# Attention's row sums: reciprocal on VectorE from PSUM in place of logarithm and exponential on ScalarE

## The reference, cut to what matters

```
log_f = log_sigmoid(f_logit + b_f);  c = cumsum(log_f)
logits = q.k / sqrt(d) + c[t] - c[s]         (causal)
probs = softmax(logits)
o = probs @ v
y = (o * silu(g)) @ w_out
```

## Time and profile before

| | us |
|---|---|
| median of 3 runs | 2958.67 (2952.82 to 2960.47) |
| the profiled execution | 2953.92 |
| its span in the trace | 2952.1 |
| TensorE busy | 2819.0 (95%) |
| VectorE busy | 1713.6 (58%) |
| ScalarE busy | 1064.9 (36%) |
| GpSimd busy | 1349.7 (46%) |

### The profile page before, as it was taken

How to read it: one execution, slowest core, us unless ns; L and a number is a source line. 1 busy time by engine, 2 the same in 40 slices (tenths; PEclk the granted TensorE clock), 3 DMA queues, 4 the chain that set the end, 5 groups by cost and what they waited for, 6 DMA issues and landing times. The chain is left out here.

```text
span 2952.1 us, 39371 instructions
## 1 busy us (share of the span) xinstructions
PE 2819.0 (95%) x13294; PEld 2181.5 (74%) x13294; DVE 1713.6 (58%) x2184; ACT 1064.9 (36%) x1407; POOL 1349.7 (46%) x1652
## 2 busy tenths in 40 slices
PE   5999999998999999999989999999999999996997
PEld 3788888866878877787778888777676777774775
DVE  7679989988262612663564223263566666667454
ACT  5343443444120100000233222132466666665232
POOL 2344544557754534445724233577422222223775
PEclk9999999999999999999999999999999999998998
DMA  7521111155321132113221111323300000000423
GB/s 301 181 70 63 63 65 67 68 182 175 136 68 54 40 131 78 43 44 106 100 93 36 37 36 36 121 95 89 116 29 30 28 28 30 32 30 8 161 81 115
DMA packets 89450, 241.15 MB, mean 82 GB/s; under 512 B 6960, under 2 KB 20352, under 8 KB 88576
## 3 DMA queue, kind: packets, MB, share of 16 engines
q1 hardware_dynamic: 59648, 172.58, 17.8%
q10 hardware_dynamic: 29696, 67.16, 6.3%
HBM read 207.20 MB, written 32.51 MB: 81 GB/s over the span
## 5 line engine op out<-in xcount | busy, mean ns | idle before, releaser
L630 PE MATMUL ps<-t_h_hi,t_wh 128*128 128x512 f32 x2464 | 1003.7, 407 | 42.9 <-POOLq L542 15.4
L632 PE MATMUL ps<-t_h_hi,t_wl 128*128 128x512 f32 x2464 | 979.5, 398 | 0.0
L631 PE MATMUL ps<-t_h_lo,t_wh 128*128 128x512 f32 x2464 | 977.6, 397 | 0.0
L534 POOL CAST t_wh<-t_wst 128x1024 fp32r<-128x1024 f32 (+2 forms) x306 | 317.6, 1038 | 1431.3 <-PE ps L632 1318.9
L539 POOL TENSOR_TENSOR t_wl<-t_wst,t_wh 128x256 fp32r<-128x256 f32 (+2 forms) x1224 | 935.7, 796 | 24.5
L630 PEld LDWEIGHTS ps<-t_h_hi,t_wh 128*128 128x128 f32 x2464 | 465.8, 189 | 199.9 <-issue 52.6
L632 PEld LDWEIGHTS ps<-t_h_hi,t_wl 128*128 128x128 f32 x2464 | 465.8, 189 | 112.9
L631 PEld LDWEIGHTS ps<-t_h_lo,t_wh 128*128 128x128 f32 x2464 | 466.3, 189 | 111.4 <-issue 6.0
L2257 DVE SCALAR_TENSOR_TENSOR ps<-t_upad,t_vec,ps 128x1024 f32<-128x1024 f32 x224 | 275.5, 1286 | 7.1 <-DVE ps L2251 0.9
L630 PE MATMUL ps<-t_y_hi,t_wh 128*128 128x512 f32 x512 | 205.1, 401 | 11.0 <-POOLq L542 8.9
L632 PE MATMUL ps<-t_y_hi,t_wl 128*128 128x512 f32 x512 | 204.0, 398 | 0.0
(11 more groups left out here) (344 smaller groups left out, 3850.7 us busy)
## 6 DMA issues: line engine op xcount, KB each, us to landing
t_wst<-w_even_in SPq DMA_DIRECT2D x40, 512.0 KB, 3.3
t_wst<-w_ple SPq DMA_DIRECT2D x64, 320.0 KB, 2.8
t_wst<-w_even_out SPq DMA_DIRECT2D x32, 512.0 KB, 3.5
t_wst<-w_fox_in SPq DMA_DIRECT2D x32, 512.0 KB, 3.5
t_modw<-w_mod SPq DMA_DIRECT2D x6, 2048.0 KB, 16.1
t_xr<-x_d ACTq DMA_DIRECT2D x6, 2048.0 KB, 13.2
t_wst<-w_gla_in SPq DMA_DIRECT2D x24, 512.0 KB, 3.6
t_wst<-w_odd_in_a SPq DMA_DIRECT2D x16, 512.0 KB, 3.5
```

What stands on the lines that cost most here:

```text
L534: pool.tensor_copy(wh[b][:, 0:w], wst[b][:, 0:w]).then_inc(S("w_high"), 1)
L630: pe.matmul(o, w1, x1, start=start and k == 0, stop=False)
L631: pe.matmul(o, w1, x2, start=False, stop=False)
L632: last = pe.matmul(o, w2, x1, start=False, stop=stop and k == kts - 1)
```

## The change

ScalarE's two operations are taken out, with their semaphore f_ln. In their place VectorE has one, `shares`, which reads bank 5 and writes the reciprocal to the same buffer as before. It stands right behind `gated` of the same half. TensorE's `weight_sums` waits for f_inv in place of f_ln. Nothing else moves.

```diff
@@ TensorE, weight_sums
-            at_least("f_ln", 2 * p + c)
+            at_least("f_inv", 2 * p + c)
@@ ScalarE
-        def sums(p, c):
-            act.wait_ge(S("f_ws"), 2 * p + c + 1)
-            act.wait_ge(S("f_pv"), 12 * p + (12 if c else 4))
-            A(share_of(c)[:, :], bank(5), ACT.Ln).then_inc(S("f_ln"), 1)
-
-        def shares(p, c):
-            act.wait_ge(S("f_ln"), 2 * p + c + 1)
-            A(share_of(c)[:, :], share_of(c)[:, :], ACT.Exp, scale=-1.0).then_inc(S("f_inv"), 1)
@@ ScalarE, window
             scores_out(p, 3, 0)
-            if carry:
-                sums(p - 1, 1)
-                shares(p - 1, 1)
             tops_out(p, 0, 0)
...
                 next_square(n, 0)
-            sums(p, 0)
             tops_out(p, 1, 1)
...
                 next_raw(n, 1)
-            shares(p, 0)
             if more:
                 next_square(n, 1)
@@ ScalarE, behind the last window
         window(7, more=False)
-        sums(7, 1)
-        shares(7, 1)
-        act.wait_ge(S("f_inv"), 16)
@@ VectorE
+        def shares(p, c):
+            dve.wait_ge(S("f_ws"), 2 * p + c + 1)
+            dve.wait_ge(S("f_pv"), 12 * p + (12 if c else 4))
+            dve.reciprocal(share_of(c)[:, :], bank(5)).then_inc(S("f_inv"), 1)
@@ VectorE, window
             below_max(p, 2, 0)
             if carry:
                 gated(p - 1, 1)
+                shares(p - 1, 1)
             below_max(p, 3, 1)
...
             gated(p, 0)
+            shares(p, 0)
             below_max(p, 7, 0)
@@ VectorE, behind the last window
         gated(7, 1)
+        shares(7, 1)
         shared(7, 1)
```

More of the change, by code:

```diff
@@ L380, in build @@
     RED = numbered((0, 0), (0, 1), (1, 1), (1, 0))
-    LN = numbered((0, 0), (1, 0))
-    INV = numbered((0, 0), (1, 0))
     YG = numbered((0, 0), (1, 0))
```

## The result

The changed kernel takes 2983.45 us (median of 4 runs, 2981.99 to 2986.45), the kernel before 2955.74 us (4 runs, 2952.73 to 2960.47). The ratio is 1.0098, 95% interval 1.0082 to 1.0114: slower by 27.7 us, where 12.5 were forecast: the right way, and more than twice the sum. (2983.45 still lies in the stated range, just under its upper end of 2984; but that range was set on a median of 2958.67 for the kernel before, and the four runs have 2955.74.)

What follows compares the result with a forecast made beforehand. TensorE was taken to bound the six loop windows, other engines window 7. Terms 8.4 + 1.0 + 3.1 = 12.5 us, set on the median 2958.67, gave 2971.2 us; range 2957 to 2984, the forecast case's own 2968 to 2976.

Steps and rivals of the forecast that it cites:

- the stated range: Forecast of the whole time: 2957 to 2984 us, taking in the upper half of the cheap case and all the dear one.
- the 18 loads and the 7 that move: ScalarE's table loads: 18 go, 23.1 us; 7 in windows 0 to 6 move to next_ln.
- place two: First half, windows 0 to 7: shared 1.4 us late, covered by 3.5 us slack in windows 0 to 6; window 7 pays.
- window 7's middle: From gated(7, 0) to TensorE's weight sums: hardly any wait to cover the reciprocal, so the whole 3.1 us is paid.
- the tail: After the last gated: 0.1 us gained, off the path as TensorE waits for GpSimd's split; counted as 0.
- Window 7's head: Carried half in window 7: ScalarE and the maxima 2.6 us late; cost taken as 1.0 us, between 0 and 2.6.
- The reciprocal's length: Each 128x512 reciprocal on VectorE out of PSUM: 3.15 us taken, between 0.77 and 8.1 us.
- the third rival: In the list of rivals: TensorE's clock falls from 2.4 to 1.2 GHz, about 18 us, 2989 us; chance 0.05.
- the second: Dearer reciprocal: eight ordinary turns an element, 4.34 us each, costing 21.5 us, 2980.2 us in all; chance 0.20.
- place one: Carried half, windows 1 to 7: delay 3.07 us less cover 1.65; six windows pay 8.4 us, window 7 1.0 us.

Runs made afterwards that it cites:

- both reciprocals hidden: Changed kernel with both reciprocals moved to stretches where VectorE waits anyway (carried one at the window's head): 2954.70 us, ratio 1.0001 to the kernel before.
- the half c = 0 alone: Changed kernel with the carried half (c = 1) back on ScalarE's logarithm and exponential, reciprocal only for c = 0: 2956.08 us, ratio 1.0009 to the kernel before.
- The variant with a buffer of its own: Changed kernel with a separate buffer for the share of c = 1, so scores_out(p, 4) no longer waits for shared(p - 1, 1): 2957.47 us, ratio 1.0007.
- the variant with the reciprocal behind the subtractions: Changed kernel with the carried reciprocal moved behind the four subtractions, right ahead of shared(p - 1, 1): 2969.12 us, ratio 1.0057 to the kernel before.
- the last variant: Changed kernel, carried reciprocal behind the four subtractions, plus two copies of the bank to an unread buffer before shared: 2977.17 us, ratio 1.0079.

## Why the prediction was wrong

**Right.** What bounds the kernel and which way it goes; that relieving ScalarE is worth nothing (period 73.20 with both reciprocals hidden); the 18 loads and the 7 that move (counts of both match; ScalarE's relief of 42.7 us was 41.0); that all hangs on the carried half, through `scores_out(p, 4)` and TensorE's scores, where most of the wait stands before unit 6 (2.64 us) and the rest before unit 7 (0.36); that place two is covered in windows 0 to 6; window 7's middle, 3.1 us forecast, 3.2 measured (3.0 with the half c = 0 alone); the tail, 0 forecast and 0.0 measured.

**Right by luck.** Window 7's head, 1.0 us forecast and 1.0 measured. The 1.0 was picked between 0 and 2.6 without a count, and the way to it went through ScalarE's late `scores_out`. The variant with a buffer of its own has no such wait and pays the same (26.47 against 26.45 us from gate to maxima), so it did not hang on that wait; in both TensorE waits some 2.7 us for VectorE's maxima, before the change 0.72. No run here isolates it further.

**The reciprocal's length**, taken as 3.15 us, is 3.35: by the three sizes 253 ns (16 columns), 1.75 us (256) and 3.35 us (512) it has the fixed part of its neighbours (0.15 us) and 6.2 ns a column; the 2.55 us of 384 columns lie on the same line. That is a fifth of a microsecond too little, 1.2 us over six windows. The Trainium skill's "repeat count of 8" ("VectorE: DVE Perf Modes", "First, the fixed hardware budget") taken as eight turns an element would have made 4.3 us. The page gives no duration, and that reading is mine; the measurement decides: a column takes as long as about six of an ordinary operation (6.24 / 1.03). (The prediction calls this case the third rival at one place; it is the second.)

**The step that failed** is the sum of place one: "3.07 - 1.65 = 1.42 us", six times 1.4. It lacked two terms.

First, 1.5 to 1.6 us a window, some 9.8 us in all. I let the work behind the reciprocal move by the reciprocal's length and keep its own. The four subtractions had ended 0.13 us before GpSimd's split began (2378.70 and 2378.83), and moved on top of it they double (the expectations call them "of 128 columns"; two of them have 384). I had read that effect in window 7, and priced it there; in the loop I did not look what GpSimd does in the microseconds into which the work was being pushed.

Second, 9.6 us for the clock. I had it as a rival with 0.05, argued away from waits of 0.80 and 1.08 us at a clock of 1.00, "near to" a stall of 1.4. For a stall of that length the argument held: with 1.16 + 0.37 us the clock stayed at 1.00 in all six windows. But the stall was 2.64 + 0.36 us, twice as long, because of the first error, and at that length the grant fell from 2.4 to 1.2 GHz in five of six windows, 0.9 to 2.9 us each. The two errors are chained: without the contention, in the variant with the reciprocal behind the subtractions, the wait is 1.63 us, the clock holds and the loss is 16.4 us by the medians, near the forecast.

So the mechanism was the right one, with 3.24 in place of 1.42 us a window, and the clock's 1.6 us a window on top.

## What to carry to other kernels

An operation put ahead of others on an in-order engine costs its length and what the pushed work meets at its new time: look at what the neighbouring engine does in the next microseconds, not only at the slack. Before moving work onto an engine, see where it idles: the same 53.7 us cost 28 us at one place and nothing when the carried half stood 20 steps earlier and the other filled a wait for TensorE. A wait that hangs on a shared buffer can be removed with a second buffer; here one tile of 2 KB a partition bought back the loop's whole loss. The better place did the same without it.

## What the hardware showed that I had not expected

- The reciprocal out of PSUM is not held up by GpSimd: 3345 to 3351 ns in all 16, also where GpSimd's conversion and its two-operand operations ran beside it, and that conversion took 1.04 us. Copies out of PSUM in the last variant took 0.63 and 0.67 us beside GpSimd's split. Operations from SBUF to SBUF do collide with it: a subtraction 128x384 took 1.09 us in place of 0.55, a copy 128x512 0.95 in place of 0.41, GpSimd's split of 256 columns 1.05 in place of 0.73, and its conversion 2.37 us where `shared`, two copies and a subtraction ran beside it.
- Not every such pair slows VectorE: behind the subtractions `shared` started 0.02 us ahead of GpSimd's last piece (2384.82 and 2384.84) and took its usual 0.69 us, while that piece took 1.25.
- TensorE's granted clock does not fall by a sure rule after waits of 2.2 to 3 us in all: in otherwise equal windows of one loop it fell in some and held in others, and the cost where it fell was 0.8 to 2.9 us.
